# Exponentials one step ahead, keys and queries ahead of the dense filler: a two-layer MLA and convolution trunk on one Trainium2 core

## The reference

```python
z = rmsnorm(h, ln_in) @ w_in                     # 416 latent columns, gates g_a and g_c, u_val, u_gate
q = (rmsnorm(c_q) @ w_q_b)                       # 8 heads, 64 plain + 32 rotary
s = (q_lat . ckv + q_rope . krope) * SCALE       # prompt: block causal; sample: 256 cached rows + 16 new
p = softmax(s);  o_a = (p @ ckv) @ w_uv          # per head
y_a = rmsnorm(o_a * silu(g_a))
u = u_val * sigmoid(u_gate)
v = silu(layernorm(depthwise_conv31(past ++ u)))
y_c = rmsnorm(v * silu(g_c))
h = h + concat(y_a, y_c) @ w_out
h = h + sigmoid(rmsnorm(h) @ w_pg) * (p_in @ w_pe)
```

## Time and profile before

| what | value |
|---|---|
| median of 3 runs | 841.51 us (840.98 to 842.02) |
| the profiled execution | 841.38 us |
| its span in the profile | 839.6 us |
| mean granted TensorE clock | 0.988 |
| PE busy | 782.7 us, 93% of the span |
| DVE busy | 572.2 us, 68% |
| ACT busy | 410.7 us, 49% |

### The profile page before, as it was taken

The page is one execution under the profiler, slowest core; times in us unless marked ns, Lnnn a source line. Parts: engine busy times, 40 slices in busy tenths (PEclk is TensorE's granted clock), DMA queues, the critical chain, the costliest instruction groups (busy, mean ns, idle before and its releaser), DMA issues.

```text
span 839.6 us, 10488 instructions
## 1 busy us (share of the span) xinstructions
PE 782.7 (93%) x3782; PEld 604.3 (72%) x3782; DVE 572.2 (68%) x1093; ACT 410.7 (49%) x944; POOL 67.9 (8%) x104
## 2 busy tenths in 40 slices
PE   5999999989998899999999999998999889999992
PEld 4789778656765578888888878775667556888881
DVE  3337968789894786546553687888898567656455
ACT  3654644644355563353374464555444547223544
POOL 5000123000000430000000012210000011000000
PEclk9999999999999999999999999999999999999996
DMA  9622222110000163322272232111000003342203
GB/s 304 182 73 75 70 66 81 33 51 25 26 1 1 34 204 114 127 76 76 78 236 66 76 91 71 54 60 51 26 26 0 1 1 117 125 135 76 76 1 125
DMA packets 40569, 65.26 MB, mean 78 GB/s; under 512 B 7774, under 2 KB 19898, under 8 KB 40502
## 3 DMA queue, kind: packets, MB, share of 16 engines
q1 hardware_dynamic: 37354, 58.45, 21.8%
q0 software_dynamic: 3104, 6.12, 2.5%
q10 hardware_dynamic: 60, 0.02, 0.0%
HBM read 57.86 MB, written 7.17 MB: 77 GB/s over the span
## 4 chain that ended last, share of the span: by engine, by line
PE 80%; DVE 9%; ACT 7%; issue 2%; DMA 1%; SPq 0%; DVEq 0%; ACTq 0%
PE acc L598 17%; PE acc L600 17%; PE acc L599 17%; PE sharedT L532 5%; PE sharedS L775 4%; PE acc L711 4%; DVE VT L1374 3%; PE sharedT L764 3%; PE sharedO L787 3%; ACT JUNK L944 2%; PE sharedT L758 2%; DVE WLO L1310 1%; PE sharedS L532 1%; PE sharedO L532 1%; ACT WHI L948 1%
## 5 line engine op out<-in xcount | busy, mean ns | idle before, releaser
L598 PE MATMUL acc<-WHI,XHI 128*128 128x512 f32 (+1 forms) x720 | 309.9, 430 | 4.3 <-DVE WLO L1310 2.3
L600 PE MATMUL acc<-WHI,XLO 128*128 128x512 f32 (+1 forms) x720 | 279.1, 388 | 0.0
L599 PE MATMUL acc<-WLO,XHI 128*128 128x512 f32 (+1 forms) x720 | 278.5, 387 | 0.0
L1374 DVE SCALAR_TENSOR_TENSOR VT<-UX,CWT,VT 128x640 f32<-128x640 f32 x240 | 211.8, 883 | 5.1
L1310 DVE SCALAR_TENSOR_TENSOR WLO<-WR,GT,WHI 128x512 fp32r<-128x512 f32 (+1 forms) x144 | 100.1, 737 | 102.6 <-ACT WHI L948 102.6
L598 PEld LDWEIGHTS acc<-WHI,XHI 128*128 128x128 f32 x720 | 135.9, 189 | 36.9 <-issue 8.3
L599 PEld LDWEIGHTS acc<-WLO,XHI 128*128 128x128 f32 x720 | 136.1, 189 | 29.3 <-issue 6.8
L600 PEld LDWEIGHTS acc<-WHI,XLO 128*128 128x128 f32 x720 | 135.5, 188 | 26.9
L948 ACT ACTIVATE WHI<-WR,GT 128x512 fp32r<-128x512 f32 (+1 forms) x144 | 94.9, 710 | 113.5 <-PE acc L600 108.8
L948 ACT ACTIVATE PT<-sharedT 128x384 f32<-128x384 f32 (+1 forms) x80 | 35.9, 448 | 69.5 <-PE sharedT L532 69.4
L787 PEld LDWEIGHTS sharedO<-V,PT 128*128 128x128 f32 x320 | 44.1, 191 | 19.9 <-issue 15.2
(11 more groups left out here) (189 smaller groups left out, 854.3 us busy)
## 6 DMA issues: line engine op xcount, KB each, us to landing
WR<-in_w_in_dram SPq DMA_DIRECT2D x32, 256.0 KB, 3.1
WR<-in_w_in_dram SPq DMA_DIRECT2D x16, 512.0 KB, 3.6
WR<-in_w_out_dram SPq DMA_DIRECT2D x16, 512.0 KB, 3.6
WR<-in_w_pg_dram SPq DMA_DIRECT2D x16, 512.0 KB, 3.5
WR<-in_w_in_dram SPq DMA_DIRECT2D x8, 416.0 KB, 3.4
residual_spill<-H SPq DMA_DIRECT2D x5, 512.0 KB, 3.5
H<-residual_spill SPq DMA_DIRECT2D x10, 256.0 KB, 3.2
H<-in_x_prompt_dram SPq DMA_DIRECT2D x4, 512.0 KB, 7.6
```

Of the source, the lines that this page charges most:

```text
L598: mm(out, hi, w_hi, start=(first and k == 0), stop=False)
L599: mm(out, hi, w_lo, start=False, stop=False)
L600: last = mm(out, lo, w_hi, start=False, stop=(final and k == 1))
L1374: ins = stt(out=out, in0=src, scalar=w, in1=out, op0=ALU.mult, op1=ALU.add)
```

## The change

Three things move, and one number changes. On ACT, `probs(n+1)` now stands directly ahead of `probs_out(n)`, at the end of step n, where it stood directly behind it, at the start of step n + 1. On PE, `keys(h+1)` and `queries(h+1)` stand directly behind the scores, ahead of the step's first filler half. On DVE, the last sample step does all four of its taps and one of the turn ahead of `queries_out(0)`; the turn's other taps are three behind `mask(NB)`, then `filler_gate("prep")` (which is `low`), then three more. The turn has 7 taps for 8, so one tap moves to the last prompt step that has any (u = 21).

```diff
-TAP["turn"] = _take(8)
+TAP["turn"] = _take(7)
...
                 if u < UNITS - 1:
                     scores(u + 1)
 
+                if i == 1 and h < HEADS - 1:
+                    keys(h + 1)
+                if i == 2 and h < HEADS - 1:
+                    queries(h + 1)
                 filler(NB + u, slice(0, 1))
...
-                if i == 1 and h < HEADS - 1:
-                    keys(h + 1)
-                if i == 2 and h < HEADS - 1:
-                    queries(h + 1)
...
+            probs(0, PAST + P)
             for s in range(NB):
-                probs(s, PAST + P)
...
+                if s < NB - 1:
+
+                    probs(s + 1, PAST + P)
                 probs_out(s, 3)
...
+            probs(NB, P)
             sample_out(NB - 1)
...
-                probs(NB + u, P * (i + 1))
...
+                if u < UNITS - 1:
+                    probs(NB + u + 1, P * ((i + 1) % 4 + 1))
                 probs_out(NB + u, i + 1)
...
-                    taps(TAP[s][:2])
+                    taps(s)
+                    taps(TAP["turn"][:1])
                     queries_out(0)
-                    taps(TAP[s][2:])
...
-            taps(TAP["turn"][:2])
             mask(NB, P, MASK[:, 512 - P:512])
-            taps(TAP["turn"][2:])
+            taps(TAP["turn"][1:4])
             filler_gate("prep")
+            taps(TAP["turn"][4:])
```

## The result

| | before | after |
|---|---|---|
| median | 841.63 us (840.98 to 842.71, 6 runs) | 845.31 us (844.58 to 845.93, 6 runs) |
| the profiled execution | 841.38 us | 845.93 us |
| its span | 839.6 us | 844.1 us |
| mean granted TensorE clock in it | 0.988 | 0.986 |

The ratio is 1.0045, with a 95% interval of 1.0034 to 1.0056: the change makes the kernel 3.7 us slower. In after the mask stands at L1433, the taps at L1379, `low` at L1315, `queries_out` at L1458.

What follows compares the result with a forecast made beforehand. PE, busy 93% of the span, was taken as the bound, so only its pauses count. Terms +1.67 + 1.5 - 1.75 - 0.2 gave +1.2 us a layer, +2.4 in all: 841.38 to 843.8 us, range 839.8 to 846.8.

Steps and rivals of the forecast that it cites:

- Exponentials ahead of the copy, in the sample steps: Sample steps s = 0, 5, 6: the PT copy stands behind one exponential on ACT, costing 0.49, 0.59, 0.59; +1.67 us a layer.
- The turn: Last sample step into the prompt: three taps behind `low` make `mask(NB+1)` later, so `scores(2)` starts later; +1.5 us a layer.
- Keys ahead of the filler half: Prompt heads: the transposes' wait for the keys' copy goes at u = 1, 9, 13, not u = 5; -1.75 us a layer.
- u = 17 to 26: Crowded prompt steps: PE gets about 1.5 us ahead, then new PT and "cv" waits; -0.2 a layer, bounds -1.1 to +0.7.
- The warning sign set for PE's waits for PT: Profile after: the prediction is wrong if PE's waits for PT sum to over 8 us.
- The clock: Half-rate stretch behind the turn's pause: taken as 0, bounds -1.7 to +0.9 us a layer.
- the swaps in the crowded steps are paid in full: Rival: u = 17 to 26 at +0.7, a little in idle steps; +2.1 to +2.5 a layer, 846 us; chance 0.17.
- The swaps are hidden: Rival: sample-step exponentials start before the tile copies end and cost zero; 840.5 us; chance within a shared 0.29.
- The half-rate stretch falls into the longer pause: Rival: the turn's pause bears the half-rate stretch, -1.7 a layer; 840.4 us, no measurable change; chance within a shared 0.29.
- The turn is cleared: Rival: high part early, `low` and six taps end before PE is free; -3.4 a layer, 834.0 us; 0.14 with mild gain.

## Why the prediction was right

The time is 1.5 us above the forecast of 843.8, inside its range and on its side. The terms compare as follows, for one layer.

1. *Exponentials ahead of the copy, in the sample steps: +1.67 forecast, +1.72 measured.* The three places and their prices held (0.49, 0.59, 0.59 against 0.47, 0.60, 0.60; 0.06 more at s = 1). The kernel without these three swaps, with sample steps at +0.00, shows that there are no others.
2. *The turn: +1.5 forecast, +1.47 measured,* and +1.48 in the kernel that changes only this. `low` waits for the high part 4.21 us (some 4 forecast), three taps follow, PE waits 3.06 (near 3 forecast). The kernel with the three taps ahead of `low` shows that their place is the cause.
3. *Keys ahead of the filler half: -1.75 forecast, -1.57 measured.* Nothing at u = 5, as forecast. The pauses vanished, but the same four pieces (scores, half, keys, `values`) take PE a little longer in the new order, from the start of the scores to that of `values` 2.54 us (208.87 to 211.41) where it was 2.43 (205.88 to 208.31), so 0.47 to 0.56 of each 0.62 is left. The half alone, behind the keys, takes 0.80 (210.61 to 211.41), where the forecast put 0.65. The rows of the scores at u = 9, before and after:

```profile
205.88 0.81 PE L775 MATMUL sharedS<-KH,QH 128*128 128x384 f32 x2
...
208.87 0.81 PE L775 MATMUL sharedS<-KH,QH 128*128 128x384 f32 x2
```

4. *u = 17 to 26: -0.2 forecast, -0.13 measured,* as a sum of the parts named: the pause at u = 21 before `queries` (near 1.1 forecast, 0.92 measured) and those before the "cv" transposes (about 0.9 forecast, 0.74 and 0.68 measured). PE is 1.71 further ahead by `scores(23)` (about 1.5 forecast) and then gives back 1.58 (1.3). The kernels with and without the exponentials part the term into a gain of 1.8 and a cost of 1.7. The forecast had called it a sum of large parts that cancel, and so it is: 3.4 us over both layers lie in it that undoing the swaps brings out. The warning sign set for PE's waits for PT, over 8 us, was passed (9.9) with the sum still right: before had 2.6 of them already, which the sign left out.
5. *The clock: 0 forecast, within -1.7 to +0.9 a layer.* This is the mis-sized term: 0 in the first layer of the profiled execution, +1.3 in the second, so +0.65 a layer on average, inside the bounds, though the second layer by itself is outside them. It makes most of what the forecast is short of that execution (2.1 us: 1.3 here, 0.5 from terms 1 to 4, 0.3 from the start-up). From the page "TensorE: Matmul & The Clock Gate" of the Trainium skill ("Part 1: The HAM clock gate"), that idleness throttles the array and activity releases it, the forecast had drawn a sum some 3 us higher. The trace agrees in the direction and with less than half of the size. That this pause is what costs the clock here is shown by the other kernels: those that shorten or split it to pieces of up to 0.91 us, or have none, have 1.00 in both layers, those with 3.1 lose in both. The size was chance in part: the three executions of after with a mean clock of 0.989 took 844.6 to 845.0 us, the three at 0.986 to 0.987 took 845.6 to 845.9, and 841.38 with the measured terms 1 to 4 alone is 844.4.

The measured terms sum to 1.72 + 1.47 - 1.57 - 0.13 = +1.49 a layer, 2.98 for two; with 1.31 for the clock and 0.27 for the start-up that is 4.56, and the spans differ by 4.5. The profiled execution is the slowest of the six of after, so the medians differ by less, 3.7.

Of the rivals, "the swaps in the crowded steps are paid in full" was nearer in time (846) than the forecast but wrong in its cause: term 4 came out as forecast. "The swaps are hidden" is refuted by the 1.72 of the sample steps. "The half-rate stretch falls into the longer pause" is refuted by both windows of after. "The turn is cleared" did not happen here, but its price, 3.4 a layer, is what `low` behind the mask then gained (3.3 in the first layer).

## What to carry to other kernels

On an in-order engine that serves two masters, put first what is waited for now, and let what waits for a late input (here `low`, for ACT's high part) stand behind the short operation that frees a bank, with all work of free choice in front of it; three of the six taps here cost 5.3 us, or nothing, by their place. An exponential of 0.59 us moved ahead of a copy cost 0.47 to 0.60 where the engine came out of a backlog, and next to nothing where it idled; a row each shows which. When a change bundles moves on several engines, price and try them one at a time: here one was worth -6.9, and the two others cost +3.8 and +4.9, so the bundle hid a gain larger than its loss. Nor do parts add up: these three sum to +1.8, the bundle cost 3.7. Most of the difference is the clock, for the exponentials by themselves split the turn's pause and won about 3 us of it back, which they did not do in the bundle.

## What was not expected of the hardware

The lost clock came in steps. Over the 25 us around and behind a turn, PEclk was 1.00, 0.93 or 0.86 in all twenty-two windows of the eleven kernels, so 0, 1.7 or 3.4 us lost, and nothing between. With no pause, or pieces of up to 0.91 us, it was 1.00 (8 windows of 8). With a pause of 1.56 to 1.59 it was 0.93 three times and 1.00 once, with nothing in the rows read here to tell the two layers of that kernel apart. With one near 3.1 it was 0.93 three times and 0.86 seven times. The first step made PE 1.3 to 1.7 us later, the second 0.7 to 1.4. The same holds between executions of one kernel: of the 22 runs of the kernel before that the second set of experiments was timed against, those with a mean clock of 0.992 took 838.4 to 838.9 us and those at 0.988 to 0.990 took 840.0 to 842.0. What decides between the steps is open, and the length of one pause does not decide it alone. In all eleven kernels PE also waits 1.71 us ahead of the attention of each layer (61.80 and 467.44 in before), longer than in the turn of before, and the clock stays at 1.00 there. The row and the window around it, in before:

```profile
61.80 0.33 PE L532 MATMUL sharedT<-IDENT,H 128*128 128x128 f32 x1 [1.71 <-ACT UX L948]
...
60.00:65.00 5.00, 3.29 (x19) 3.18 (x19) 4.09 (x6) 3.45 (x9) 0.00 (x0) 1.00 0.35 107
```

In the turn, the pause of before thus costs its own 1.75 us and, most times, about 1.6 more, and its removal gives back both: 3.3 to 3.4 a layer.

The start of the kernel, up to the first sample scores, varied by up to 2.0 us between profiles of kernels that are the same there; it is taken out wherever kernels are laid over each other here.
